# A new order of the four attention branches in a two-layer mixer kernel: D, B, A, C in place of D, B, C, A

## What is computed

```
u = RMSNorm(h); proj = u @ w_in[layer]                 # one projection, split by columns
A: q = (rms_norm(c_q) @ w_uq), k, v = rms_norm(c_kv) @ w_ukv, rotary parts; softmax(q k) v, 4 heads
B: dilated sliding window, three patterns merged; softmax(q k + bias) v, 4 heads
C: an indexer (8 heads) picks the top 128 keys of each row; softmax over them, 4 heads
D: two softmax maps for each head, p0 - lambda * p1, times v, then rms_norm, 4 heads
y = concat(A, B, C, D, each * silu(gate)) @ w_out[layer]; h = h + RMSNorm(y)
```

## Time and profile before

| | before |
|---|---|
| median of 3 runs | 719.69 us |
| lowest and highest | 718.64 and 719.76 us |
| the profiled execution, its own time | 717.92 us |
| the profiled execution, span of its instructions | 716.1 us |
| TensorE busy | 676.5 us (94%) |
| VectorE busy | 432.3 us (60%) |
| ScalarE busy | 330.3 us (46%) |
| GpSimd busy | 242.1 us (34%) |
| mean granted clock of TensorE | 0.976 |

### The profile page before, as it was taken

The page is one execution under the profiler, slowest core; times in us unless marked ns, Lnnn a source line. Parts: engine busy times, 40 slices in busy tenths (PEclk is TensorE's granted clock), DMA queues, the critical chain, the costliest instruction groups (busy, mean ns, idle before and its releaser), DMA issues. The chain is left out here.

```text
span 716.1 us, 10494 instructions
## 1 busy us (share of the span) xinstructions
PE 676.5 (94%) x3840; PEld 545.0 (76%) x3840; DVE 432.3 (60%) x1068; ACT 330.3 (46%) x751; POOL 242.1 (34%) x209
## 2 busy tenths in 40 slices
PE   6999999999999998799999999999999999978996
PEld 4888887887897754369998897788889776445896
DVE  4313897899797554640470269888978865456114
ACT  5424535653434637742353264465533354666121
POOL 1432633335055612002424536125323663200030
PEclk9999999999999969999999999999999997899999
DMA  8458876332322101112363598442322221030202
GB/s 249 131 176 244 231 215 237 95 107 67 111 85 85 59 1 58 60 27 95 118 177 110 178 257 230 123 132 74 105 75 74 79 70 59 0 118 1 90 28 91
DMA packets 66644, 80.96 MB, mean 113 GB/s; under 512 B 10737, under 2 KB 52337, under 8 KB 66593
## 3 DMA queue, kind: packets, MB, share of 16 engines
q1 hardware_dynamic: 66593, 80.29, 36.6%
HBM read 69.76 MB, written 13.93 MB: 117 GB/s over the span
## 5 line engine op out<-in xcount | busy, mean ns | idle before, releaser
L652 POOL TENSOR_TENSOR w_low<-w_raw,w_high 128x512 fp32r<-128x512 f32 (+2 forms) x156 | 199.2, 1309 | 383.2 <-ACT w_high L692 383.2
L1184 PE MATMUL bank<-uT,w_high 128*128 128x512 f32 x400 | 160.0, 400 | 0.2 <-DVE staging L998 0.2
L1186 PE MATMUL bank<-uT,w_low 128*128 128x512 f32 x400 | 158.3, 396 | 0.0
L1185 PE MATMUL bank<-uT,w_high 128*128 128x512 f32 x400 | 158.1, 395 | 0.0
L800 ACT ACTIVATE probs<-probs,negmax 128x128 f32<-128x128 f32 (+3 forms) x160 | 89.1, 559 | 95.7 <-DVE negmax L1039 95.4
L1184 PEld LDWEIGHTS bank<-uT,w_high 128*128 128x128 f32 x400 | 75.5, 189 | 18.6 <-issue 1.3
L1186 PEld LDWEIGHTS bank<-uT,w_low 128*128 128x128 f32 x400 | 75.4, 189 | 17.8
L1185 PEld LDWEIGHTS bank<-uT,w_high 128*128 128x128 f32 x400 | 75.5, 189 | 16.2
L692 ACT ACTIVATE w_high<-w_raw 128x2048 fp32r<-128x2048 f32 (+2 forms) x39 | 72.7, 1865 | 26.1 <-DMA w_raw<-in_w_out 23.1
L1184 PE MATMUL bank<-w_high,mix 128*128 128x256 f32 x256 | 72.4, 283 | 1.0 <-DVE mix L1124 1.0
L1186 PE MATMUL bank<-w_high,mix 128*128 128x256 f32 x256 | 71.6, 280 | 0.0
(11 more groups left out here) (150 smaller groups left out, 1089.4 us busy)
## 6 DMA issues: line engine op xcount, KB each, us to landing
w_raw<-in_w_in SPq DMA_DIRECT2D x27, 1024.0 KB, 5.4
w_raw<-in_w_out SPq DMA_DIRECT2D x8, 1024.0 KB, 4.9
parts_dram<-staging SPq DMA_DIRECT2D x12, 512.0 KB, 4.9
strips<-strips_dram SPq DMA_DIRECT2D x24, 256.0 KB, 4.4
dqk<-parts_dram SPq DMA_DIRECT2D x24, 256.0 KB, 4.4
hX<-in_x SPq DMA_DIRECT2D x8, 512.0 KB, 6.0
qidx<-parts_dram SPq DMA_DIRECT2D x12, 256.0 KB, 4.2
w_raw<-in_w_in SPq DMA_DIRECT2D x4, 512.0 KB, 5.4
```

The costliest lines, as they stand in the source:

```text
L652: ins = nc.gpsimd.tensor_tensor(w_low[:, s, ks, 0:w], w_raw[:, s, ks, 0:w], w_high[:, s, ks, 0:w].bitcast(F32), ALU.subtract)
L1184: nc.tensor.matmul(out_ap, lh, rh, start=start, stop=False)
L1185: nc.tensor.matmul(out_ap, lh, rl, start=False, stop=False)
L1186: return nc.tensor.matmul(out_ap, ll, rh, start=False, stop=stop)
```

## The change

- The branches run in the order D, B, A, C; jobs 8 to 11 are A and 12 to 15 are C. A's units move from the lines of jobs 8 to 11 to those of jobs 4 to 7, and C's query, key and gate units from the lines of jobs 4 to 7 to those of jobs 8 to 14. The units of B's values move to the lines of jobs 3 and 4. The column groups are loaded in the new order.
- A's sums of squares (`asums`) are made inside the last unit of B's values: before each of its eight blocks there is one single-column matmul. GpSimd first adds the two pieces of the query latents' squares, so there are eight such matmuls in place of twelve. `asums` has a unit number and a work bank of its own, and its bank is released by VectorE at `aup_head`, as before.
- D's eight tiles are issued in groups of 3, 3 and 2, in place of 2, 3, 2 and 1.
- The units `bq 0` and `gc 1` can be made in two halves (`part`).
- The residual rows `hX` lie in the memory of the gates. They are loaded after all `mix` steps, at `y01`, in place of `norm 12`. `mix` is split over two memories, A's query and key memory and C's are exchanged, and values and D's output get room of their own.
- `ya` is cut up: two more blocks of the output product are done before the last job ends. Three late weight groups get fixed steps for their conversion.

```diff
-BRANCHES = "DBCA"
+BRANCHES = "DBAC"
...
-    scores 0 0 2, topk 2, unit gd 1, scores 0 2 5, unit gb 0, scores 0 5 7, topk 1, scores 0 7 8
...
-    scores 3 0 2, norm 2, topk 3, unit bk 0, turn 2 0, turn 2 1, scores 3 2 5, topk 2, unit bk 1, scores 3 5 7, pv 1, turn 2 2, turn 2 3, scores 3 7 8, dsquares 0
-    scores 4 0 2, norm 3, dscale 0, topk 1, unit cqq 0, turn 3 0, turn 3 1, scores 4 2 4, dnorm 0, pv 2, topk 2, turn 3 2, turn 3 3, topk 2, norm 4
...
-    scores 9 0 2, norm 8, unit ga 1, pv 5, turn 8 0, turn 8 1, scores 9 2 4, mix 6, aup_head
-    scores 10 0 2, norm 9, turn 8 2, turn 8 3, aup 0, aup 1, turn 9 0, turn 9 1, scores 10 2 4, aturn 0, turn 9 2, turn 9 3
-    scores 11 0 2, norm 10, aup 2, aturn 1, aup 3, pv 6, turn 10 0, turn 10 1, scores 11 2 4, aturn 2, aturn 3, mix 7, turn 10 2, turn 10 3
-    scores 12 0 2, norm 11, scores 12 2 4, turn 11 0, turn 11 1, turn 11 2, turn 11 3
-    scores 13 0 2, norm 12, scores 13 2 4, pv 7, mix 3, mix 2, turn 12 0, turn 12 1, turn 12 2, turn 12 3
...
+    scores 0 0 3, topk 3, unit gd 1, scores 0 3 6, topk 2, unit gb 0, scores 0 6 8, topk 2, unit gb 1
+    scores 1 0 3, norm 0, topk 1, unit ckv 0, scores 1 3 6, topk 1, turn 0 0, turn 0 1, part bq 0, scores 1 6 8, topk 1, unit bq 0, turn 0 2, turn 0 3
...
+    scores 3 0 3, norm 2, topk 1, unit bk 1, scores 3 3 6, topk 2, turn 2 0, turn 2 1, unit bv 0, unit bv 1, scores 3 6 8, pv 1, topk 1, turn 2 2, turn 2 3, dsquares 0, squares_a
+    scores 4 0 2, norm 3, dscale 0, topk 2, unit bv 2, turn 3 0, turn 3 1, scores 4 2 4, dnorm 0, asums, unit bv 3, pv 2, topk 2, turn 3 2, turn 3 3, aup_head
+    scores 5 0 2, norm 4, topk 2, unit ga 0, turn 4 0, turn 4 1, pv 3, scores 5 2 4, aup 0, dsquares 1, topk 1, turn 4 2, turn 4 3
+    scores 6 0 2, norm 5, dscale 1, topk 1, aup 1, unit ga 1, dnorm 1, turn 5 0, turn 5 1, scores 6 2 4, aturn 0, topk 3, turn 5 2, turn 5 3, aup 2
+    scores 7 0 2, norm 6, aturn 1, topk 1, pv 4, aup 3, turn 6 0, turn 6 1, scores 7 2 4, aturn 2, topk 2, turn 6 2, turn 6 3, aturn 3
+    scores 8 0 2, norm 7, topk 3, unit cqq 0, turn 7 0, turn 7 1, scores 8 2 4, topk 1, turn 7 2, turn 7 3
...
+    scores 13 0 2, norm 12, part gc 1, pv 7, turn 12 0, turn 12 1, scores 13 2 4, fill 15, mix 2, turn 12 2, turn 12 3
+    scores 14 0 2, norm 13, unit gc 1, turn 13 0, turn 13 1, scores 14 2 4, mix 3, turn 13 2, turn 13 3
+    scores 15 0 2, norm 14, pv 8, ya 0 0 4, mix 0, turn 14 0, turn 14 1, scores 15 2 4, mix 1, turn 14 2, turn 14 3, ya 0 4 6, norm 15, mix 4, ya 2 0 6, turn 15 0, turn 15 1, ya 1 0 3, turn 15 2, turn 15 3, ya 1 3 6, pv 9, mix 5
...
-    if k == "aup_head":
-        return ["dve", "dve"]
+    if k in ("asums", "aup_head"):
+        return ["dve"]
...
-        hX = at("hX", "X", [P, NB, DM], F32)
+        hX = at("hX", "gate", [P, NB, DM], F32)
...
+                if step[0] == "squares_a":
+                    pool.wait_ge(lat_squared, l + 1)
+                    nc.gpsimd.tensor_tensor(sq[0:QL - P, 0, :], sq[0:QL - P, 0, :], sq[0:QL - P, 1, :], ALU.add
+                                            ).then_inc(lat_summed, 1)
...
+                    sums = step == ("unit", "bv", NB - 1)
+                    if sums:
+                        pe.wait_ge(lat_summed, l + 1)
+                        sums_bank = work_bank(l * NU + UNIT_AT[("asums",)])
...
+                        if sums:
+                            part, tb = 2 * (k // NB), k % NB
+                            ins = nc.tensor.matmul(sums_bank[:, k:k + 1], sq[:, part, tb * P:(tb + 1) * P], ones[:],
+                                                   start=True, stop=True)
```

137 lines of the change are left out of this document (74 added, 63 removed).

## The result

The changed kernel took 768.59 us (median of 4 executions, 764.71 to 769.88) beside 719.73 us for the kernel before in the same measurement: a ratio of 1.0691, 95% interval 1.0649 to 1.0734. I had forecast 722.7 us and a range of 712 to 732. The direction that I called likeliest, slower, was right; the size is far outside the range.

The account below looks back on a forecast made before the run. TensorE, busy nearly all the time, was taken to set the length. Per layer 15.2 - 6.6 - 2.0 - 1.5 - 3.2 = +1.9 us; two layers less 0.8 give +3.0, so 722.7 us, range 712 to 732.

Parts of the forecast that it names:

- The four waits: TensorE waiting for VectorE at `turn 3 0`, `unit bv 3`, `aup_head` and `unit ga 1`: 3.0, 2.1, 3.9, 5.1 us, together 14.1.
- The second: Wait at `unit bv 3`, whose bank is that of `dnorm 0`, which VectorE must have read: 2.1 us.
- The smaller waits: `aup 2`, `aturn 1` and `aturn 3` waiting for ScalarE: 1.7 us a layer (0 to 3).
- The lines of jobs 12 to 15: C's gate units and more output product fill most idle time there: -6.6 us a layer (-8.9 to -4.6).
- The new wait for `mix 1`: In the last jobs' lines, `ya 0 4 6` waits for `mix 1`: between nothing and 1.9 us, and a little more.
- D's tiles: Groups of 3, 3, 2 remove TensorE's waits, 0.8 of 2.8 us left: -2.0 us a layer (-2.8 to 0).
- The sums: Eight single-column sums cost 2.0 us where twelve took 3.47: -1.5 us a layer (-2.6 to -1.2).
- The clock: Old low clock gone, worth -6.3, less 1.0 for each of three new waits: -3.2 us a layer (-6.3 to 0).
- the old fall: Kernel before, layer 1: low clock from 252.0 us, 13.7 us long after twelve single-column matmuls; loss of 6.3 us a layer.
- the signs that I listed: Changed profile: idle at four waits, idle from 283 us under half, no single-column stretch, clock 0.50 only briefly behind those waits.
- My slow rival: The low clock stays: waits paid in full or sums still lower it; +3.2 us a layer, 729.1 us; chance 0.17.
- 731 us: Time by the skill's rule: all four waits paid with 1.8 us each, 7.2 a layer against the 6.3 before.

Follow-up runs that it names:

- The mended order: Changed kernel with the lines of jobs 3 to 6 reordered so VectorE is not late at the four places, three top-k rounds moved to jobs 8 and 9: 731.44 us.
- e11_mended_spare: Changed kernel with jobs 3 to 9 reordered, plus nine dense spare matmuls over the 1.01 us wait ahead of `unit bv 3`: 726.76 us, ratio 1.0104.
- the last version: Kernel before with twelve sums amid `ga 1`, squares and weight folding early, `aup 0` ahead of norm 9, `mix 6` behind `aup 1`: 715.01 us, ratio 0.995.

## Why the prediction was wrong

**The four waits: right.** 12.8 us found for 14.1 forecast. The second was 0.94 for 2.1: the clock had fallen by then, and TensorE took 5.2 us from `turn 3 0` to the wait instead of 2.8, so VectorE caught up. The smaller waits (0.88, 0.87 and 0.76 us for `aup 2`, `aturn` and a turn) make 2.5 for 1.7. The mended order, the same work in another order, shows what these waits were worth with all that hung on them: 37 us.

**The lines of jobs 12 to 15: right in kind, smaller.** The idle time shown fell from 8.8 to 75.0 - 70.44 = 4.6 us, 4.2 for the 6.6 forecast. The new wait for `mix 1` was 2.05 us, at the upper end of what I gave it. But there is low clock now in these lines too, 0.89 over the stretch.

**D's tiles: wrong in sign.** The step "the new grouping always has its banks free" did not hold for thirds in the old lines, where the wait grew to 2.93 us. In the changed kernel the time went elsewhere: 5.4 us idle in place of 2.2, so +3.2 a layer and not -2.0. `part bq 0`, which I let wait up to 1 us, waited 2.60. Its weights landed late enough that ScalarE waited 2.07 us for them, and GpSimd's conversion ran from 121.98 to 127.86. At `turn 1 0` TensorE waited 2.20 us because the four products of norm 1 took 4.98 us beside GpSimd's conversion, which started at 138.29. The timelines of VectorE and GpSimd:

```profile
139.63 4.98 DVE L958 SCALAR_TENSOR_TENSOR probs<-probs,coef,probs 128x128 f32<-128x128 f32 x4
...
156.85 1.94 DVE L958 SCALAR_TENSOR_TENSOR probs<-probs,coef,probs 128x128 f32<-128x128 f32 x4
...
138.29 5.25 POOL L663 TENSOR_TENSOR w_low<-w_raw,w_high 128x512 fp32r<-128x512 f32 x4 [10.43 <-ACT w_high L707]
```

The same four products took 1.94 us for norm 2. I had priced that sharing for `dsquares` and not for the norms.

**The sums: right at the high clock.** In the run where it held (e11_mended_spare), a unit of values with eight sums takes eight steps of 0.59 us, 4.7 us, against 2.9 without: 1.8 for the 2.0 forecast.

**The clock: the step that failed.** I wrote that the sums "can no longer fill a stretch alone", counted the old fall as gone, and priced the waits at 1.0 a piece, -3.2 a layer in all. Of the 13.6 us that TensorE is busy longer in layer 1, and the 1.5 that fewer sums should have saved, all is the clock: some +15 in place of -3.2, a miss of 18 us a layer and most of the 46 us by which the forecast fell short. The stretch of 30.7 us is about half of the low clock in layer 1. The rest is 3.4 us among D's jobs, 6.8 at `ga 1`, and 6.8, 3.4 and 6.8 in the lines of jobs 12 to 15, where I had counted none. Of the signs that I listed the four waits came, and "the clock at 0.50 only for short stretches behind those waits" did not. Three parts of that step were wrong.

- The waits don't have a fixed price. I took one row, a fall of 3.6 us behind a wait of 1.2 us, as the size of a fall. Behind the wait of 3.10 us it was 30.7 us.
- What stands behind the wait sets how long the fall lasts. Sums amid dense matmuls do no harm by themselves (full clock in `ga 1` with twelve, in `bv 3` with eight once the wait of 1.01 us was covered), but with a wait of 1.0 to 2.5 us ahead of the same units the clock was low for 13.6 to 20.5 us. In the changed kernel they stood right behind two waits, with a third behind them. Without seven of the sums the stretch was 10.3 us.
- The terms are not additive. I summed waits and falls apart; the kernel puts wait, wait, sums, wait and wait into some 50 us. The 6.3 us of the old fall could be had, as the run with no fall between 249 and 270 us shows, only where no wait took its place.

My slow rival was the nearest in kind. Its "every wait is paid in full" and "the sums still bring the clock down" were set side by side as alternatives, where the runs show the two together: a wait brings the clock down, and the sums behind it keep it there. And its amount was wrong. It let the clock give nothing back, +3.2 a layer. It had no case in which the clock costs more than before, though the walk through the list had just found 14 us of new waits. The Trainium skill, TensorE: Matmul & The Clock Gate, "HAM oscillation — how this bites in real kernels", from which I had worked out 731 us, points the right way: idle gaps between bursts brought the low clock back in both layers, at `turn 3 0` and at `ga 1` each time. The price that I took with it, 1.8 us a gap, was again my row's.

Each kernel has one profiled execution, and the same program can fall differently from one to the next: beside these runs the kernel before took from 712.29 us (mean granted clock 0.981) to 723.16 us (0.967). So the medians carry the comparisons, and the length of a single fall is that of one execution.

Left open: why the same wait is followed by 3.4 us at the low clock in one layer and by 10.2 in the other, why a wait of 1.43 us in the last version brought a fall and in the kernel before none, whether dense matmuls keep the clock up in a block of sums at all, and how many that would need.

## What to carry to other kernels

When a reordering puts waits on TensorE, don't price the clock as a fee for each wait: look at what runs behind it, and expect narrow matmuls there to stretch a fall over the whole unit and on to the next wait, as they did here. Price new waits and falls jointly, with an upper bound from the longest low stretch that the kernel could chain together. And before moving a step ahead of TensorE's bulk work, write down for each waiting bank how many microseconds of VectorE's list stand ahead of its release: here that walk gave 14.1 us for the four waits where 12.8 were found, and a list written with it took 37 us off the changed kernel.
